# Attention heads mixed in pairs, with the latent heads' preparation moved off GpSimd

## The reference, cut to what matters

```python
for l in range(DEPTH):                      # 2 layers
    h = rms_norm(x, attn_norm_g[l])
    c_q, c_kv, k_rope, gq, gk, gv, pool_in, gate_logits = split_columns(h @ w_in[l], IN_SIZES)
    o_mla = mla_branch(c_q, c_kv, k_rope, ...)   # 8 "latent" heads: q, k of 96 = 64 + 32 rotary, v of 64
    o_gqa = gqa_branch(gq, gk, gv, ...)          # 8 "grouped" heads of 64, 2 key/value heads
    o_pool = pool_branch(pool_in, ...)           # window means of 2, 4, 8, 16 tokens, less the token
    gates = sigmoid(gate_logits)                 # 3 x 1024 columns
    merged = (gates[0] * (o_mla @ w_branch_mla[l]) + gates[1] * (o_gqa @ w_branch_gqa[l])
              + gates[2] * (o_pool @ w_branch_pool[l]))
    x = x + merged @ w_out[l]
    ...                                          # feed-forward part
# a head, of either kind: p = softmax(q k^T * scale) over 256 keys;  o = p v
# latent q and k are normed per head, then their last 32 elements are rotated by tables
```

## Time and profile before

| | us |
|---|---|
| median of 3 runs | 1616.69 |
| lowest, highest | 1611.17, 1620.07 |
| the profiled execution | 1614.02 |
| its span in the trace | 1612.2 |
| heads' stage, each of two layers | 116.78 |
| TensorE busy over the span | 1537.8 |
| VectorE busy over the span | 1044.6 |

### The profile page before, as it was taken

How to read it: one execution, slowest core, us unless ns; L and a number is a source line. 1 busy time by engine, 2 the same in 40 slices (tenths; PEclk the granted TensorE clock), 3 DMA queues, 4 the chain that set the end, 5 groups by cost and what they waited for, 6 DMA issues and landing times.

```text
span 1612.2 us, 23627 instructions
## 1 busy us (share of the span) xinstructions
PE 1537.8 (95%) x9984; PEld 1379.2 (86%) x9984; DVE 1044.6 (65%) x1453; ACT 824.8 (51%) x1173; POOL 132.3 (8%) x132
## 2 busy tenths in 40 slices
PE   6989998999999899989999999899999997899997
PEld 5968898999888689889988987899878886799886
DVE  5795586788568755767865665666458557566446
ACT  4444554656454445455654465555446456455444
POOL 1182000000013900000000000000001000000000
PEclk9999999999999999999999999999999999999999
DMA  6431244545454223535454532455555541354551
GB/s 245 168 112 70 105 165 150 190 177 208 173 186 170 79 79 135 184 126 208 159 209 168 221 130 79 151 196 190 189 180 189 198 167 51 125 190 176 209 185 51
DMA packets 38297, 255.71 MB, mean 159 GB/s; under 512 B 4528, under 2 KB 5552, under 8 KB 8752
## 3 DMA queue, kind: packets, MB, share of 16 engines
q1 hardware_dynamic: 37904, 253.77, 43.3%
q10 hardware_dynamic: 288, 0.43, 0.1%
HBM read 253.14 MB, written 1.05 MB: 158 GB/s over the span
## 4 chain that ended last, share of the span: by engine, by line
PE 86%; DVE 8%; ACT 4%; POOL 1%; issue 1%; DMA 0%; ACTq 0%; DVEq 0%
PE psum L919 14%; PE psum L921 14%; PE psum L922 14%; PE psum L928 12%; PE psum L932 12%; PE psum L930 12%; PE psum L882 4%; PE psum L1056 2%; DVE w_low L1640 2%; PE psum L1025 2%; PE psum L1113 1%; ACT w_high L1260 1%; POOL stat L2113 1%; DVE stat L1800 1%; DVE head_work L1810 1%
## 5 line engine op out<-in xcount | busy, mean ns | idle before, releaser
L1640 DVE TENSOR_TENSOR w_low<-w_raw,w_high 128x1024 fp32r<-128x1024 f32 (+1 forms) x476 | 572.9, 1218 | 294.8 <-ACT w_high L1260 294.4
L1260 ACT ACTIVATE w_high<-w_raw 128x1024 fp32r<-128x1024 f32 (+1 forms) x476 | 495.6, 1050 | 365.1 <-PE psum L932 219.9
L919 PE MATMUL psum<-x_high,w_high 128*128 128x256 f32 x1600 | 463.6, 290 | 2.7 <-DVE x_low L1649 2.7
L921 PE MATMUL psum<-x_low,w_high 128*128 128x256 f32 x1600 | 457.0, 286 | 0.0
L922 PE MATMUL psum<-x_high,w_low 128*128 128x256 f32 x1600 | 456.4, 285 | 0.0
L919 PEld LDWEIGHTS psum<-x_high,w_high 128*128 128x128 f32 x1600 | 311.5, 195 | 9.3 <-issue 8.2
L921 PEld LDWEIGHTS psum<-x_low,w_high 128*128 128x128 f32 x1600 | 311.8, 195 | 0.4
L922 PEld LDWEIGHTS psum<-x_high,w_low 128*128 128x128 f32 x1600 | 311.4, 195 | 0.0
L928 PE MATMUL psum<-w_high,ff_high 128*128 128x512 f32 x256 | 99.8, 390 | 0.0
L930 PE MATMUL psum<-w_low,ff_high 128*128 128x512 f32 x256 | 99.6, 389 | 0.0
L932 PE MATMUL psum<-w_high,ff_low 128*128 128x512 f32 x256 | 99.6, 389 | 0.0
(11 more groups left out here) (257 smaller groups left out, 2506.8 us busy)
## 6 DMA issues: line engine op xcount, KB each, us to landing
w_raw<-in_weights SPq DMA_DIRECT2D x230, 1024.0 KB, 4.8
w_raw<-in_weights SPq DMA_DIRECT2D x4, 832.0 KB, 5.9
rows<-in_second_rows SPq DMA_DIRECT2D x4, 512.0 KB, 4.4
w_raw<-in_weights SPq DMA_DIRECT2D x2, 768.0 KB, 4.1
residual<-in_x SPq DMA_DIRECT2D x2, 512.0 KB, 6.6
w_raw<-in_weights SPq DMA_DIRECT2D x2, 512.0 KB, 3.8
out<-residual SPq DMA_DIRECT2D x2, 512.0 KB, 2.7
dil_masks<-in_consts SPq DMA_DIRECT2D x1, 576.0 KB, 5.6
```

What stands on the lines that cost most here:

```text
L919: eng.matmul(o, wh[:, j, cut], high[:, k, :], start=k == 0 and f % 2 == 0, stop=False, skip_group_check=True)
L921: eng.matmul(o, wh[:, j, cut], low[:, k, :], start=False, stop=False, skip_group_check=True)
L1260: act(self.unit_view(self.wh, u), raw, ACT.Copy).then_inc(sem("w_high"), 1)
L1640: tt(self.unit_view(self.wl, u), raw, self.unit_view(self.wh, u), ALU.subtract).then_inc(sem("w_low"), 1)
```

## The change

The heads are taken two at a time: eight pairs, 0 to 3 grouped, 4 to 7 latent. Iteration n holds `p_turn` of pair n-1 (eight transposes, banks 6 and 7), `scores` of pair n (banks 4 and 5, one to a head), its exponentials, a gates unit A, `av` of pair n-1 with the two heads' matmuls alternating (bank 6) and `head_out`, the turn of two latent heads' keys (`mla_turn_k`, bank 7, taken by VectorE), `p_norm` of pair n itself, a unit B, the turn of two latent heads' queries (`mla_turn_q`, bank 7, taken by ScalarE), a piece of the preparation, and in pairs 0 to 3 a unit C. That is the same 20 units. The turns of latent heads stand in iterations 3 to 6. Semaphores now count heads twice a step.

The preparation moves: the copy and the squares to ScalarE (`mla_square`, iteration 0), scaling and rotation to VectorE (iterations 1 and 2), window sums and means to VectorE (4 and 5, with the 1/w and the subtraction in one instruction); the roots stay on GpSimd. `take_gates` no longer waits for the windows, which now use scratch memory.

At the end the last pair's `p_turn` is followed by two units of branch_gqa and then by its `av`; `pool_mix` comes behind them.

```diff
@@ Plan.mixing
-        n_heads = GQA_H + MLA_H
-        for n in range(n_heads + 3):
-            if n >= 3:
-                add("av", l, n - 3)
-                if (n - 3) % 2:
-                    add("head_out", l, n - 3)
-            if 2 <= n < n_heads + 2:
-                add("p_turn", l, n - 2)
-            if 1 <= n < n_heads + 1:
-                add("p_norm", l, n - 1)
-            if n < n_heads:
-                add("scores", l, n)
-                self.prefetch(self.n_used)
-                add("p_exp", l, n)
-            kind = next(prepare, None)
-            if kind:
-                add(kind, l)
-            next(gates)
+        n_pairs, first = (GQA_H + MLA_H) // 2, GQA_H // 2
+        prepare = {0: ("mla_square", "mla_rstd_k", "mla_rstd_q"), 1: ("mla_scale_k", "mla_rotate_k"),
+                   2: ("mla_scale_q", "mla_rotate_q"), 4: ("window_sum",), 5: ("window_mean",)}
+        for n in range(n_pairs):
+            if n:
+                add("p_turn", l, n - 1)
+            add("scores", l, n)
+            self.prefetch(self.n_used)
+            add("p_exp", l, n)
+            next(gates)
+            if n:
+                add("av", l, n - 1)
+                add("head_out", l, n - 1)
+            if first <= n + 1 < n_pairs:
+                add("mla_turn_k", l, n + 1 - first)
+            add("p_norm", l, n)
+            next(gates)
+            if first <= n + 1 < n_pairs:
+                add("mla_turn_q", l, n + 1 - first)
+            for kind in prepare.get(n, ()):
                 add(kind, l)
-            next(gates)
+            if n < first:
+                next(gates)
         for _ in gates:
             pass
+        add("p_turn", l, n_pairs - 1)
         add("gate_sigmoid", l, 1, 0)
+        gqa = self.linear("branch_gqa", l, lambda panel: add("gated", l, 1, panel))
+        next(gqa)
+        next(gqa)
+        add("av", l, n_pairs - 1)
+        add("head_out", l, n_pairs - 1)
...
@@ mixing_memory
-            m["prob"], m["probt"] = work[0:3], [work[3], self.scr[:, 3 * PANEL:4 * PANEL]]
+            m["prob"] = [work[0:2], work[2:4]]
+            m["probt"] = [self.scr[:, i * PANEL:(i + 1) * PANEL] for i in (3, 7)]
@@ tensor
+            elif kind in ("mla_turn_k", "mla_turn_q"):
...
+                q.wait_ge(sem(f"m_{what}_rotated"), at("mla_rotate_" + what, l))
+                acquire(b)
+                for i in range(2):
+                    for t in range(TT):
+                        o = i * SEQ + t * P
+                        d = turn(bank[b][0:MLA_QK, o:o + P], tok[:, t, 2 * p + i, :])
...
             elif kind == "scores":
...
+                for i in range(2):
+                    acquire(4 + i)
+                    for t in range(TT):
+                        d = eng.matmul(bank[4 + i][:, t * SEQ:(t + 1) * SEQ], qt[i][:, t * P:(t + 1) * P], kt[i],
+                                       start=True, stop=True)
+                    d.then_inc(sem("scored"), 1)
...
             elif kind == "p_turn":
...
+                for i in range(2):
+                    prob = self.mix[l]["prob"][n % 2][i]
+                    q.wait_ge(sem("p_normed"), 2 * (at("p_norm", l, n) - 1) + i + 1)
+                    acquire(6 + i)
...
+            elif kind == "av":
...
+                for kt in range(TT):
+                    for i in range(2):
...
+                        d = eng.matmul(bank[6][HD * i:HD * i + HD, 0:SEQ], val, m["probt"][i][:, kt * SEQ:(kt + 1) * SEQ],
+                                       start=kt == 0, stop=kt == TT - 1, skip_group_check=True)
...
@@ scalar
+            elif kind == "mla_square":
...
+                q.step(act(m["mk"][:, :, :, NOPE:], kr, ACT.Copy))
+                q.settle()
+                for place, tile in enumerate((m["mk"], m["mq"])):
+                    o = self.scr[:, 2 * UNIT * place:2 * UNIT * place + n]
+                    act(o.rearrange("p (t h d) -> p t h d", t=TT, h=MLA_H), tile, ACT.Square
+                        ).then_inc(sem("m_squared"), 1)
+            elif kind == "mla_turn_q":
...
+                act(self.mix[l]["qk"][0:MLA_QK, 2 * p:2 * p + 2, :],
+                    bank[7][0:MLA_QK, :].rearrange("p (k s) -> p k s", k=2), ACT.Copy,
+                    scale=self.first_col(l, "q_head_g")[0:MLA_QK, :]).then_inc(sem("m_q_taken"), 1)
@@ vector
+            elif kind in ("mla_scale_k", "mla_scale_q"):
...
+                q.step(tt(tile, tile, r.to_broadcast([P, TT, MLA_H, MLA_QK]), ALU.mult))
+            elif kind in ("mla_rotate_k", "mla_rotate_q"):
...
+                rotate(tile, MLA_H, ROPE, self.mix[l]["t" + what], [tile], f"m_{what}_rotated")
+            elif kind == "window_sum":
+                self.window_sums(q, eng, key[0])
+            elif kind == "window_mean":
+                self.window_means(q, eng, key[0])
...
-                if panel >= 3:
-                    q.wait_ge(sem("window_mixed"), at("mla_f", l))
...
             elif kind == "p_norm":
                 l, n = key
+                for i in range(2):
+                    st, prob = self.head_stat(n, i), self.mix[l]["prob"][n % 2][i]
+                    q.wait_ge(sem("exp_done"), 2 * (at("p_exp", l, n) - 1) + i + 1)
...
@@ gpsimd
-            elif kind == "mla_a":
...
-            elif kind == "mla_f":
...
-                rotate(self.mix[l]["mq"], self.mix[l]["tq"], "m_q_rotated")
-                self.window_sums(q, eng, l)
+            elif kind in ("mla_rstd_k", "mla_rstd_q"):
```

More of the change, by code:

```diff
@@ L398, in mixing @@
             add("pool_mix", l, n)
-        self.whole("branch_gqa", l, lambda panel: add("gated", l, 1, panel))
+        for _ in gqa:
+            pass
         self.whole("branch_pool", l, lambda panel: add("gated", l, 2, panel))
@@ L1022, in tensor @@
-                b = 4 + n % 2
-                acquire(b)
-                for t in range(TT):
-                    d = eng.matmul(bank[b][:, t * SEQ:(t + 1) * SEQ], qt[:, t * P:(t + 1) * P], kt, start=True,
-                                   stop=True)
-                d.then_inc(sem("scored"), 1)
-                free[b] = (sem("exp_done"), at("p_exp", l, n))
+                    halves = [slice(HD * i, HD * i + HD) for i in range(2)]
+                    qt = [m["gh"][half, n, :] for half in halves]
@@ L2246, in window_sums @@
             for a, c0 in ((POOL_PAD, 0), (SEQ, POOL_PAD)):
[L2247 removed]
+                part = tmp[n % 2][:, n, a:a + POOL_PAD]
                 q.step(tt(part, part, edge[:, n, c0:c0 + POOL_PAD], ALU.mult))
```

267 lines of the change are left out of this document (108 added, 159 removed).

## The result

The changed kernel takes 1568.64 us (median of 4, 1565.64 to 1570.48) against 1616.42 for the kernel before (4 runs, 1611.17 to 1620.07): ratio 0.9705, 95% interval 0.9688 to 0.9721. Predicted were 1569.0. The profiled execution took 1568.98 us, its span is 1567.2. The executions of the kernel before scatter by up to 15 us (1605.45 to 1620.80 over all runs of it), those of the changed kernel by 7 (1565.64 to 1572.86), so a hit within half a microsecond is in part luck.

A forecast was written before the change was run, and what follows sets the result against it. TensorE, busy 95% of the span, was taken as the bound. Each layer's stage falls from 116.78 to 92.3 us, 49 in two layers, taken as 48: 1566 against the profiled execution, 1569 against the median; range 1561 to 1577.

The forecast's parts named there:

- TensorE's own work: Heads' stage: a pair's av takes one head's 1.01 us, its grouped scores 1.06, saving some 12.3 us a layer.
- The blocks: Heads' stage: TensorE's blocks in the changed order, start to start, sum to 91.8 us; periods 12.1 and 11.0.
- The bank 7 wait: Latent pairs 4 to 6: TensorE waits for ScalarE's copy of the turned queries, 0.4 to 0.5 us each.
- Waits and clock, 12.5 a layer: Heads' stage: TensorE's waits and the low clock behind them do not come back, some 12.5 us a layer.
- Late VectorE: Rival: less slack, two pairs a layer end in a wait with low clock behind, 14 us in all: 1583; chance 0.17.
- Slower, VectorE the bound: Rival: VectorE becomes the bound, deciding at 14.6 us a pair; at 15.6 the whole takes 1633; chance 0.05.
- Strict order: Rival: second head's passes start only after the first's last; pair's scores 1.7 us, av about 1.3: 1579; chance 0.08.
- no overlap: Rival: a pair's halves run one after the other, 12.3 us a layer come back: 1594; chance 0.07.
- GpSimd's roots: Two roots left on GpSimd hold VectorE up by nothing; a contrary rule would add up to 2 x 2.9 us.
- The sum by the row: The forecast total that counts the roots at nothing, following a trace row where VectorE's split kept its 1.22 us.
- The whole: Both layers' heads' stages together save 48 us, giving a median of 1569.

The follow-up runs named there:

- e3: Changed kernel, but TensorE waits for the first head's passes before the second's in grouped scores and every av, av written head after head: 1595.62 us.
- e6: Changed kernel with the latent keys' turn right behind the scores and the queries' turn behind av, a gates unit behind each: 1562.85 us.
- e9: Kernel before, heads one at a time, with the preparation off GpSimd and spread one piece per head: 1606.91 us, ratio 0.9957.
- e2: Changed kernel with squares, scaling, rotations and windows back on GpSimd in the same steps: 1575.82 us.
- e1: Kernel before, heads one at a time, with squares moved to ScalarE and scaling, rotations and windows to VectorE in the same steps: 1616.18 us, ratio 1.0004.
- e10: Changed kernel with 3 added products of 512 elements on VectorE in front of each pair's norms: 1588.28 us.
- e11: Changed kernel with 6 added products of 512 elements on VectorE in front of each pair's norms: 1625.51 us, ratio 1.0061 to the kernel before.
- e8: Changed kernel with av written head after head, no wait between the heads: 1570.31 us.
- e12: The e6 kernel run once more, unchanged: 1564.21 us.
- e5: The changed kernel itself run again, nothing altered: 1570.78 us.

## Why the prediction was right, and where it was not

- **TensorE's own work.** Predicted 12.3 a layer from 1.01 and 1.06 per pair. The rows have 1.01 and 1.07, e3 gives 13.1 without its gaps and 13.7 with them. Right in mechanism and size.
- **The blocks.** Stage 91.8 forecast, 90.9 measured; periods 12.1 and 11.0, measured 11.96 and 10.98. Latent scores 1.54 + changes of shape, 1.73 on the chain. Right.
- **The bank 7 wait.** 0.4 to 0.5 in three pairs: 0.43 three times. e6 takes it away, 3.5 us in all.
- **Waits and clock, 12.5 a layer.** The size was right: 25.1 and 24.5 in all, less 13.1, leave 12.0 and 11.4. The cause was half right, and this is the weakest step of the prediction. It laid the norm's wait to GpSimd's hold, and put the waits for exponentials into the same sum without asking what they waited for. The runs part it: taking GpSimd's work away gives 5.6 and 4.8 with single heads (e9) and 4.8 with pairs (e2). The other 6.4 and 6.6 I lay to the latent transposes in banks 4 and 5, which the change has put one pair at a time into bank 7, with units between. In the first layer this agrees with e9: 4.0 of waits and 3.5 of clock, less the 1.3 of waits that the changed kernel has itself, are 6.2. But the share is a difference of runs; no run moved those transposes alone. That these waits went although nobody had asked for their cause was luck. And the moves are worth something only where VectorE has room: e1 gained nothing.
- **Late VectorE.** Maxima in pair 3 began at 116.22, 1.7 behind the scores' end, and no wait came of it: right. The slack behind the norms was 1.5 us in a latent pair, where 1.2 to 1.5 were forecast: right. Pair 2 was forecast to hold VectorE 12.6 us; from its first maxima (103.31) to the next (116.22) are 12.9, of which VectorE waited 1.0, so it was 11.9. The tighter one was pair 1: 11.85 us from 91.46 to 103.31 without a wait, since the sums for the roots reach 0.9 us into it. The forecast looked at pair 2 alone and did not see that pair 1 has no idle time to catch up in. That no wait came of it owes something to luck. The rival's price, 14 us for two waits a layer, is near to what e10 shows (17.8 in the two stages for 2.1 us more).
- **Slower, VectorE the bound.** Deciding point 14.6 us a pair, 1633 at 15.6. e11 has 11.75 + 4.2 = 15.95 in pair 1 and took 1625.51; e10, at 13.9, lost 18 us and still beat the kernel before. The mechanism is real. Its waits begin between 11.75 and 13.9, near the period of 11.96, and the whole gain is lost between 13.9 and 15.95, where the forecast had put it at 14.6.
- **Strict order, no overlap.** e3 speaks against the second; e8, and the order of the records in the grouped scores, against the first.
- **GpSimd's roots.** While they ran in the changed kernel (89.13, 92.41) VectorE's splits took their 1.22, as in the earlier trace rows; e2 shows it once more. The sum by the row was right.
- **The whole.** Forecast 48 in the two stages; measured 49.6, of which 1.5 are lost again behind them and 2.7 in the dilated stage at a low clock that comes and goes from run to run: with 0.3 more behind it, 45.1 between the two profiled executions, 47.8 between the medians. So the stages gave 1.6 more than forecast and the rest took 4.5 back; the forecast of the median is right, and that it is right to 0.4 us is luck.

## What to carry to other kernels

Write work that leaves half of the array idle in pairs of different halves, next to each other; their written order within the pair did not matter here. Before an engine takes work over from another, add up its idle time period by period, not over the stage or at one wait: pair 1 had 0.2 us left while the stage had 15, and 2 us more a pair cost 18. And for every wait ask first which buffer it is for: 5.4 of the 7.1 us of waits here stood at transposes that borrowed the banks of scores just written, and 3.6 of them stayed when GpSimd's work was gone (e9).

## What the runs showed of the hardware that was not expected

- Passes for the other half of the rows or columns run beside the first head's although all of the first head's are written ahead of them: of eight passes of grouped scores the last ones of the two heads are the seventh and eighth to start, of eight latent ones the fourth and eighth (changed kernel). In e8 the passes of av start in couples 13 ns apart.
- Beside GpSimd's products of 1536 elements two norm instructions took 3.14 us in place of 0.62 (e2, 99.39); beside its power of 16 elements, 2.90 us long, a split kept its 1.22 (96.60). An instruction on two elements a partition took 1.24 us in place of 0.17 beside GpSimd's sum of 1084 elements (before, 116.19).
- The clock in a stage that no kernel here touches differs between executions of the same kernel: 1.00 and 0.91 over the same 40 us (e6, e12), 0.91 and 0.96 (changed, e5). In the aligned traces of before and changed this is 2.7 us, beside the 3.5 that e6 gained in the stages.
